# Two-layer decoder step on one core: the normalized rows kept in feature order, and the gather's weights loaded with a step of eight elements

## The chip, the cores and the metric

The kernel runs on one core of one Trainium2 chip. Its time is the device time of one execution in microseconds (us). Three executions of the kernel before took 1154.89, 1151.49 and 1144.73 us; their median, 1151.49 us, is the time before. A fourth execution was profiled. It took 1148.22 us, and its trace spans 1146.3 us from the first to the last instruction.

## The reference, cut to what matters

The model is one inference step with two layers: RWKV-7 time mixing, then differential attention, each followed by a mixture of 16 experts of which every token uses two. There are 336 tokens (272 of a prompt with its meta tokens, 64 of eight samples), a model width of 1024 and an expert width of 512, all in float32.

```python
x = _layernorm(DEEPNORM_ALPHA * x + h, post_ln[l, 0, 0], post_ln[l, 0, 1])
x = _layernorm(DEEPNORM_ALPHA * x + _moe(x, router_w, router_b, w_gate[l], w_up[l], w_down[l]), ...)

# _moe: gates are zero but for the two chosen experts of a token
for e in range(N_EXPERTS):
    h = jax.nn.silu(xt @ w_gate[e]) * (xt @ w_up[e])
    y = y + gates[:, e:e + 1] * (h @ w_down[e])
```

The change touches the way in which the normalized rows `xt` reach the experts, in both layers.

## The kernel before, in words

The program is written out engine by engine, with semaphores between them; the order on each engine is the order of its code. TensorE is PE in the profile (its weight loads are PEld), VectorE DVE, ScalarE ACT, GpSimd POOL. SP issues the weight transfers.

In each layer the 336 token rows lie in `YT`, tokens on the partitions in three tiles `t` (128, 128 and 80 rows) and 1024 features along each row. After the first layer norm (`normalize`, L2423) three things happen. PE turns the rows (L1356) for the router; ACT and DVE copy the turned rows out (`turned_copy`); and the router's small chain on DVE chooses the experts, which ends in `select`, a 0/1 matrix `SelF` that says which token goes into which of 64 places of an expert (L2460).

Beside this the rows are split into a high and a low part, `XTM[0]` and `XTM[1]`, of the type that PE multiplies in one pass (fp32r). ACT writes the high parts (`normed_copy`, L1851: tile 0 between the turned copies, tiles 1 and 2 after the router's sigmoid). The low parts, row minus high part, are written by POOL for tile 0 (`remainder`, L690) and by DVE for tiles 2 and 1 (L2515), right after `select`.

`gather` (L1212) multiplies them with `SelF`. It takes four experts at a time (a quad): for each of 8 chunks of 128 features there are 6 matmuls (two parts by three tiles), each with 128 columns of `XTM` as the stationary weights and 256 columns of `SelF` moving. A quad therefore has 48 matmuls, a layer 192, the program 384. A `gather` call takes two chunks (12 matmuls), and its result is moved out of PSUM by ACT or DVE with scale and bias (`gathered`). The four calls of a layer's first quad run before its first pair of experts; each later quad is gathered inside the loop over the eight pairs, two calls (24 matmuls) in each of the pairs 0 to 5 (`more_rows`).

A chunk's 128 features are not neighbours. The experts' weights come in with feature 8p+k on partition p, chunk k, because that makes each partition's part of a transfer contiguous. So chunk k of the gather must hold features k, k+8, k+16 and so on. Before the change the split copies do this: they write `XTM` chunk by chunk, so that consecutive features of a row land 128 elements (512 bytes) apart, and the gather's weights are 128 consecutive elements.

The weights of the experts use seven slots of 2 MB in SBUF. SP issues a half slot (1 MB) as soon as the pair that used it has finished that half (`free`, waiting for `gate_mm`, `up_mm`, `down_mm` of PE). A pair needs six slots, and PE works through a pair as gate, up, gather or scatter, turn, down.

Of the kernel before, what the change touches and what calls it, by code (L numbers as in the profile page):

```python
# [8 lines left out]
ALU = mybir.AluOpType  # L9
ACT = mybir.ActivationFunctionType  # L10
AX = mybir.AxisListType.X
F32 = mybir.dt.float32
# [4 lines left out]
P = 128  # L17
D = 1024
NC = D // P
# [20 lines left out]
QUAD = 4 * SLOTS  # L40
# [104 lines left out]
def build(nc, I, O, const, at):  # L145
    ctx = ExitStack()
    with ctx:
        sems = {}

        def S(name):  # L150
            name = SHARED.get(name, (name, 0))[0]
            if name not in sems:
                sems[name] = ctx.enter_context(nc.semaphore(name))
            return sems[name]

        A = ctx.enter_context(nc.sbuf_tensor("arena", [P, ARENA], F32))
        ps = ctx.enter_context(nc.psum_tensor("ps", [P, 8, 512], F32))
# [6 lines left out]
        def cut(n, where=None):  # L164
            if where is not None:
                return A[:, where:where + n]
            v = A[:, top[0]:top[0] + n]
            top[0] += n
            assert top[0] <= ARENA, top
            return v  # L170
# [31 lines left out]
        YT = cut(3 * D)  # L202
        xT = chan(YT[:, 0:NC * T])
        YT = YT.rearrange("p (t n) -> p t n", t=3)
# [40 lines left out]
        o = SLOT  # L245
# [3 lines left out]
        def rc(name):  # L249
# [28 lines left out]
        XTM = [[nc.alloc_sbuf_tensor_at(f"xtm_{part}{t}", [P, D], FR, offset=arena_at + 4 * (base + NC * T + D * (3 * i + t)))[:, :]  # L278
                for t in range(3)] for i, part in enumerate(("hi", "lo"))]
# [121 lines left out]
        def rx_part(i, h, c):  # L401
            return (rx_lo_[i] if h else rx_hi_)[c // 4][:, T * (c % 4):T * (c % 4) + T]

        def x_part(place, h, c):
            return PX[place][c // 4][h][:, T * (c % 4):T * (c % 4) + T]

        def bank(b, n=512):
            return ps[:, b, 0:n]

# [20 lines left out]
        def sums_bank(lv, hf):  # L430
            return (0, 2)[(lv + 1) % 2] + hf
# [197 lines left out]
        def _(pool):  # L629
# [55 lines left out]
            def remainder(l):  # L685

                pool.wait_ge(S("xtm_hi"), 3 * l + 1)
                lo, hi = [XTM[h][0].rearrange("t (k p) -> t p k", k=NC) for h in (1, 0)]
                pool.tensor_tensor(lo, YT[:, 0, :].rearrange("t (p k) -> t p k", k=NC), hi.bitcast(F32), ALU.subtract
                                   ).then_inc(S(f"first_lo{l}"), 1)  # L690

            pool.wait_ge(S("wkvp_ready"), after("wkvp_ready", 1))
# [13 lines left out]
            for hp in range(2):  # L706
                pool.memset(QZ[hp][64 * (1 - hp):64 * (1 - hp) + 64], 0.0)
                i = pool.drain()
# [56 lines left out]
        def _(pe):  # L765
            prime(pe, "pe")
            def mm(out, lhsT, rhs, start=True, stop=True):
                return pe.matmul(out, lhsT, rhs, start=start, stop=stop)  # L768

            def three(out, x, w, start, stop):  # L770

                mm(out, x[0], w[0], start, False)
                mm(out, x[1], w[0], False, False)
                return mm(out, x[0], w[1], False, stop)
# [7 lines left out]
            for t in (1, 0, 2):  # L782
                t0, n = TOK[t]
# [3 lines left out]
                for hf in range(2):  # L787
                    for c in range(4):
                        i = pe.transpose(ps[:, 1 + 2 * t + hf, n * c:n * c + n],
                                         xrow[0:n, t, P * (4 * hf + c):P * (4 * hf + c) + P], ident[0:n, 0:n])  # L790
# [63 lines left out]
            for i in range(3):  # L854
                for co in range(NC):
                    n = 8 * i + co
# [4 lines left out]
                    for k in range(NC):  # L861
                        if co == 0:
                            pe.wait_ge(S("rx_hi"), 8 * i + k + 1)
                            pe.wait_ge(S("rx_lo"), 8 * i + k + 1)
                        m = three(bank(n % 4, T), [PWR[n % 2][h][:, P * k:P * k + P] for h in range(2)],
                                  [rx_part(i, h, k) for h in range(2)], k == 0, k == NC - 1)
# [164 lines left out]
            for k in range(NCH):  # L1031
# [3 lines left out]
                for lv in range(1, LEVELS[k]):  # L1035
                    for hf in range(2):
# [3 lines left out]
                        for c in range(4 * hf, 4 * hf + 4):  # L1040
                            for hp, q in enumerate(QH):
                                m = mm(ps[QH[1 - hp], sums_bank(lv, hf), 64 * (c % 4):64 * (c % 4) + 64], LM[q, c, :], XU[k % 2][q, c, :])
                        m.then_inc(S("y_mm"), 1)
                    beside(k, lv)
                    for hf in range(2):
                        pe.wait_ge(S("y_ready"), product_at(k, lv, hf))
                        b = products_bank(lv, hf)
                        for c in range(4 * hf, 4 * hf + 4):
# [4 lines left out]
                            for hp, q in enumerate(QH):  # L1053
                                m = mm(ps[QH[1 - hp], b + 1, cols], XI[q, c, :], YI[q, c, :])
# [42 lines left out]
            for c in range(NC):  # L1097
                if c % 2 == 0:
                    pe.wait_ge(S("sq_a"), after("sq_a", c // 2 + 1))
                m = variances(c, slice(0, 256))  # L1100
# [12 lines left out]
            for c in range(NC):  # L1113
                if c % 4 == 0:
                    pe.wait_ge(S("sq_b"), after("sq_b", c // 4 + 1))
                m = variances(c, slice(256, T))
# [94 lines left out]
            def gather(q, i, order):  # L1211

                for h, t in order:
                    t0, k = TOK[t]
                    for c in (2 * i, 2 * i + 1):
                        o = QUAD * (c % 2)
                        m = mm(ps[:, i % 2, o:o + QUAD], XTM[h][t][0:k, P * c:P * c + P],
                               SelF[q % 2][0:k, t].rearrange("p e s -> p (e s)"), h == t == 0 and c == 2 * i, h == t == 1 and c == 2 * i + 1)
                if order[-1] == (1, 1):
                    m.then_inc(S("xg_mm"), 1)  # L1220

            def more_block(n0, n):
                pe.wait_ge(*over("o_sel", n, 1))
                for c in range(NC):
                    for t, (t0, k) in enumerate(TOK):
                        for h in range(2):
                            m = mm(ps[:, c // 4, P * (c % 4):P * (c % 4) + P], XTM[h][t][0:k, P * c:P * c + P],
                                   SelO[0:k, t, :], t + h == 0, t + h == 3)
                m.then_inc(S("o_pe"), 1)
                pe.wait_ge(*over("o_xg", n, 1))  # L1230
                pe.wait_ge(*over("o_weights", n, 48))
                for k in range(2):
                    w = w_in(n0 + 6 * (PAIRS - 1) + 3 + k)
                    for c in range(NC):
                        m = mm(bank(2 + k), oXg[:, c, :], w[:, c, :], c == 0, c == NC - 1)
                m.then_inc(S("o_pe"), 1)
                pe.wait_ge(*over("o_h", n, 1))
                for f in range(NF):
                    pe.transpose(ps[:, 2, P * f:P * f + P], HH[:, P * f:P * f + P], ident)
                for t, (t0, k) in enumerate(TOK):  # L1240
                    pe.transpose(ps[:, 3, t0:t0 + k], SelO[0:k, t, :].bitcast(F32), ident[0:k, 0:k])
                for t, (t0, k) in enumerate(TOK):
                    m = mm(ps[:, 3, 400:401], SelO[0:k, t, :].bitcast(F32), gtp[0:k, t:t + 1], t == 0, t == 2)
                m.then_inc(S("o_pe"), 1)
                pe.wait_ge(*over("o_ht", n, 1))
                w = w_down(n0 + 6 * (PAIRS - 1) + 5)
                for hf in range(2):
                    for f in range(NF):
                        m = mm(bank(4 + hf), oHT[:, P * f:P * f + P], w[:, f, 512 * hf:512 * hf + 512], f == 0, f == NF - 1)
                m.then_inc(S("o_pe"), 1)  # L1250
                pe.wait_ge(*over("o_y", n, 1))
                for t, (t0, k) in enumerate(TOK):
                    for hf in range(2):
                        if t:
                            pe.wait_ge(*over("o_add", n, 2 * t + hf - 1))
                        mm(ps[0:k, 6 + hf, :], oSG[:, t0:t0 + k], oYY[:, 512 * hf:512 * hf + 512]).then_inc(S("o_pe"), 1)
# [166 lines left out]
            for t, (t0, n) in enumerate(TOK):  # L1423
                pe.wait_ge(S("ln_x"), 3 + t + 1)
                for c in range(NC):
                    m = pe.transpose(ps[:, c, t0:t0 + n], YT[0:n, t, P * c:P * c + P], ident[0:n, 0:n])
# [181 lines left out]
        def _(act):  # L1608
            prime(act, "act")
            def f(out, in_, func, **k):  # L1610
                return act.activation(out, in_, func, **k)  # L1611
# [35 lines left out]
            for i, t in enumerate((1, 0, 2)):  # L1647
                t0, n = TOK[t]
# [116 lines left out]
            for n in range(24):  # L1765
                i, c = n // 8, n % 8
# [79 lines left out]
            def normed_copy(l, t):  # L1846

                n = TOK[t][1]
                if l == 0 and t == 0:
                    act.wait_ge(S("out_wkvp"), 32)  # L1850
                f(XTM[0][t][0:n, :].rearrange("t (k p) -> t p k", k=NC), YT[0:n, t, :].rearrange("t (p k) -> t p k", k=NC),  # L1851
                  ACT.Copy).then_inc(S("xtm_hi"), 1)

            def turned_copy(l, t):

# [106 lines left out]
            for i, X in enumerate((aKT, aVT, QZ)):  # L1962
                for c in range(NC):
# [8 lines left out]
                    else:  # L1972
                        if c == 0:
                            act.wait_ge(S("q_zero"), after("q_zero", 1))
                        for hp in range(2):
                            q = slice(64 * hp, 64 * hp + 64)
                            n = 32 * c + 16 * (c % 2) + SS * hp
                            copy(X[hp][q, c, :], ps[q, c % 4, 0:2 * P])
                            m = copy(Qbd[q, :, n:n + SS], ps[q, c % 4, 2 * P:T].rearrange("p (u n) -> p u n", n=SS))
# [91 lines left out]
        def _(dve):  # L2071
            prime(dve, "dve")
            tt, tsc, stt, cp = dve.tensor_tensor, dve.tensor_scalar, dve.scalar_tensor_tensor, dve.tensor_copy
# [9 lines left out]
            for i, t in enumerate((1, 0, 2)):  # L2083
                t0, n = TOK[t]
# [418 lines left out]
            def experts(l, n0):  # L2503
# [6 lines left out]
                def remainder(t):  # L2510

                    n = TOK[t][1]
                    dve.wait_ge(S("xtm_hi"), 3 * l + t + 1)
                    lo, hi = [XTM[h][t][0:n, :].rearrange("t (k p) -> t p k", k=NC) for h in (1, 0)]
                    tt(lo, YT[0:n, t, :].rearrange("t (p k) -> t p k", k=NC), hi.bitcast(F32), ALU.subtract).then_inc(S("xtm_lo"), 1)  # L2515

                def folded(t):

# [104 lines left out]
                for t in range(3):  # L2623
                    m = with_gains(t, ALPHA)
# [28 lines left out]
            for co in range(1, 24):  # L2653
# [3 lines left out]
                if 2 <= co < 5:  # L2657
                    m = with_gains(co - 2, 1.0)
# [38 lines left out]
            for u in range(NU + 2):  # L2697
                if u < NU:
                    t, h = units[u]
# [8 lines left out]
                if 1 <= u <= NU:  # L2708
                    t, h = units[u - 1]
                    nk = P * t + P  # L2710
                    st, p = st4[(u - 1) % 2], PP[(u - 1) % 3]
# [14 lines left out]
            for i in range(UNITS):  # L2726
                b = i + 2 - TAIL // SS
                n = TAIL if i < TAIL // SS else TS
# [56 lines left out]
            for t in range(3):  # L2785
                n = TOK[t][1]
                stt(centred[0:n, t, :], YT[0:n, t, :], lsum[1][0:n, t:t + 1], GB[0:n, 0, :], ALU.add, ALU.mult)
            for t in range(3):
                n = TOK[t][1]
# [32 lines left out]
```

## Time and profile before

| what | before |
|---|---|
| median of three runs | 1151.49 us |
| the profiled execution, its own time | 1148.22 us |
| its span, first to last instruction | 1146.3 us |
| PE busy | 1031.3 us, 90% |
| DVE busy | 531.3 us, 46% |
| ACT busy | 361.8 us, 32% |
| POOL busy | 72.1 us, 6% |
| expert stage of layer 0, from the first gather to the last add | about 387 to 622 us |
| expert stage of layer 1 | about 897 to 1132 us |

The busy time of an engine is the union of its instructions' durations. A matmul's duration includes the time in which the next one already runs, so the distance between two starts, and not the duration, tells how fast a row of matmuls goes. PEclk is the granted clock: 1.00 stands for 2.4 GHz and 0.50 for 1.2 GHz.

### The profile page before, as it was taken

The page shows a single profiled execution, that of the slowest core. Times are in us where ns is not written, and L with a number is a line of the kernel's source. Part 1 is how long each engine was busy: PE and PEld are TensorE (multiplying, and loading weights), DVE is VectorE, ACT ScalarE, POOL GpSimd, SP SyncE. Part 2 cuts the span into 40 slices and gives each one's busy share as a digit, 9 for nine tenths or more (in the row PEclk, how much of TensorE's full clock was granted, in tenths as well). Part 3 has the DMA queues.
Part 4 walks back from the last instruction along what each step waited for, and adds up shares of the span by engine and source line. Part 5 has one row for each costly group of instructions (what it writes and reads, how often), then busy time and mean ns, then how long its engine had stood idle before and what let it go on. Part 6 is the DMA issues. An engine that isn't in the chain of part 4 may idle for free.

```text
span 1146.3 us, 23962 instructions
## 1 busy us (share of the span) xinstructions
PE 1031.3 (90%) x10421; PEld 719.2 (63%) x10422; DVE 531.3 (46%) x1043; ACT 361.8 (32%) x734; POOL 72.1 (6%) x103
## 2 busy tenths in 40 slices
PE   5999868998998699999997899998788699999994
PEld 4888867888866444444444899876556445454532
DVE  6866546665676621212124744565445612121215
ACT  3436435443443311111113534463324211111112
POOL 3002000010000100000000011202001000000000
PEclk9999979999999899999999999999879799999998
DMA  9703020013205899999999415535745199999992
GB/s 314 263 16 74 11 59 4 4 40 114 93 2 198 362 397 423 423 423 422 421 418 387 179 37 191 186 133 192 265 177 219 53 424 423 421 423 423 423 411 91
DMA packets 58109, 273.31 MB, mean 238 GB/s; under 512 B 5185, under 2 KB 7754, under 8 KB 33938
## 3 DMA queue, kind: packets, MB, share of 16 engines
q1 hardware_dynamic: 48112, 237.45, 51.7%
q0 software_dynamic: 9264, 33.97, 9.2%
q8 instruction: 85, 1.39, 0.5%
q10 hardware_dynamic: 626, 0.32, 0.1%
q14 instruction: 22, 0.18, 0.0%
HBM read 265.29 MB, written 6.46 MB: 237 GB/s over the span
## 4 chain that ended last, share of the span: by engine, by line
PE 76%; DVE 10%; DMA 7%; issue 3%; ACT 3%; DVEq 1%; ACTq 0%; POOLq 0%; POOL 0%
PE ps L768 70%; DMA arena<-in_moe_w_up 5%; PE ps L912 1%; ACT arena L1611 1%; PE ps L1483 1%; DMA arena<-in_cache_k 1%; DVE arena L2100 1%; DMA arena<-in_const 1%; DVE arena L2408 1%; PE ps L1191 1%; PE ps L1308 1%; ACT arena L1614 1%; PE ps L1356 1%; DVE arena L2239 0%; DVE arena L2238 0%
## 5 line engine op out<-in xcount | busy, mean ns | idle before, releaser
L768 PE MATMUL ps<-arena 64*64 64x64 f32 (+11 forms) x7576 | 580.8, 317 | 44.0 <-DVE arena L2595 10.8
L768 PEld LDWEIGHTS ps<-arena 64*64 64x64 f32 (+4 forms) x7576 | 321.3, 138 | 280.3 <-issue 218.0
L1614 ACT COPY arena<-ps 128x512 f32<-128x512 f32 (+7 forms) x308 | 126.2, 430 | 305.6 <-PE ps L768 159.8
L2490 DVE TENSOR_TENSOR arena<-arena,ps 128x512 f32<-128x512 f32 x16 | 17.4, 1084 | 164.5 <-PE ps L768 164.5
L1611 ACT ACTIVATE arena<-ps,arena 128x256 f32<-128x256 f32 (+4 forms) x98 | 46.2, 504 | 125.0 <-PE ps L768 95.0
L2501 DVE SCALAR_TENSOR_TENSOR yy_lo<-ps,arena,yy_hi 128x512 fp32r<-128x512 f32 x32 | 22.7, 747 | 123.1 <-ACT yy_hi L1611 123.1
L1611 ACT ACTIVATE pw_hi<-arena 128x1024 fp32r<-128x1024 f32 x40 | 42.3, 1058 | 89.7 <-PE ps L768 89.7
L768 PE MATMUL ps<-px_hi,pw_hi 128*128 128x336 f32 x192 | 62.7, 327 | 3.5 <-DVE px_lo L2326 2.5
L768 PE MATMUL ps<-px_lo,pw_hi 128*128 128x336 f32 x192 | 60.9, 317 | 0.0
L768 PE MATMUL ps<-px_hi,pw_lo 128*128 128x336 f32 x192 | 60.7, 316 | 0.0
L1611 ACT ACTIVATE yy_hi<-ps,arena 128x512 fp32r<-128x512 f32 x32 | 20.5, 685 | 106.3 <-PE ps L768 106.3
L1611 ACT ACTIVATE arena<-arena 128x1 f32<-128x1 f32 (+7 forms) x71 | 43.1, 642 | 20.5 <-DVE arena L2397 16.3
L2315 DVE TENSOR_TENSOR pw_lo<-arena,pw_hi 128x1024 fp32r<-128x1024 f32 x24 | 29.4, 1225 | 43.1 <-ACT pw_hi L1611 43.0
L768 PE MATMUL ps<-yy_hi,sg 128*128 128x512 f32 (+1 forms) x96 | 40.4, 420 | 5.0 <-DVE arena L2477 2.7
L768 PE MATMUL ps<-pw_hi,px_hi 128*128 128x512 f32 (+1 forms) x96 | 40.7, 424 | 3.0 <-DVE px_lo L2326 3.0
L2475 DVE TENSOR_TENSOR arena<-arena,ps 128x512 f32<-128x512 f32 (+1 forms) x48 | 32.5, 684 | 23.4 <-PE ps L768 23.4
L1611 ACT ACTIVATE arena<-ps 128x512 f32<-128x512 f32 (+4 forms) x23 | 11.4, 506 | 100.3 <-PE ps L768 100.2
L2106 DVE TENSOR_TENSOR pwr_lo<-arena,pwr_hi 128x1024 fp32r<-128x1024 f32 x24 | 29.4, 1223 | 28.4 <-ACT pwr_hi L1611 28.1
L768 PE MATMUL ps<-rx_hi_hi,pwr_hi 128*128 128x336 f32 x96 | 33.4, 347 | 9.5 <-ACT rx_hi_hi L1611 4.5
L768 PEld LDWEIGHTS ps<-px_hi,pw_hi 128*128 128x128 f32 x192 | 36.2, 188 | 5.0 <-issue 2.8
L768 PE MATMUL ps<-pw_hi,px_lo 128*128 128x512 f32 (+1 forms) x96 | 39.2, 408 | 0.0
L768 PE MATMUL ps<-pw_lo,px_hi 128*128 128x512 f32 (+1 forms) x96 | 39.0, 406 | 0.0
(230 smaller groups left out, 1378.3 us busy)
## 6 DMA issues: line engine op xcount, KB each, us to landing
arena<-in_moe_w_gate SPq DMA_DIRECT2D x64, 1024.0 KB, 15.3
arena<-in_moe_w_up SPq DMA_DIRECT2D x64, 1024.0 KB, 18.2
arena<-in_moe_w_down SPq DMA_DIRECT2D x64, 1024.0 KB, 17.4
arena<-in_rwkv_w_rkv SPq DMA_DIRECT2D x5, 2048.0 KB, 20.8
arena<-in_w_kv_shared SPq DMA_DIRECT2D x4, 2048.0 KB, 20.2
arena<-in_cache_k POOLq DMA_DIRECT2D x16, 512.0 KB, 4.5
arena<-in_cache_v POOLq DMA_DIRECT2D x16, 512.0 KB, 6.6
arena<-in_rwkv_w_out SPq DMA_DIRECT2D x2, 2048.0 KB, 10.7
```

Source lines behind the costliest of these rows:

```text
L768: return pe.matmul(out, lhsT, rhs, start=start, stop=stop)
L912: m = pe.transpose(ps[:, b + hf, P * c:P * c + P], src[:, 4 * hf + c, o0:o0 + P], ident)
L1191: m = pe.transpose(ps[0:n, 4 + g % 4, P * c:P * c + P], X[:, 4 * hf + c, t0:t0 + n], ident)
L1308: m = pe.transpose(ps[:, 2, P * f:P * f + P], HH[:, P * f:P * f + P], ident)
L1356: m = pe.transpose(ps[:, 2 * t + hf, n * c:n * c + n], YT[0:n, t, P * (4 * hf + c):P * (4 * hf + c) + P], ident[0:n, 0:n])
L1611: return act.activation(out, in_, func, **k)
L1614: return act.copy(out, in_)
L2106: tt(lo, w_in(L_RKV + n // 4)[:, :, P * (n % 4):P * (n % 4) + P], hi.bitcast(F32), ALU.subtract).then_inc(S("rw_lo"), 1)
L2315: tt(lo, w_in(L_KV + co // 4)[:, :, P * (co % 4):P * (co % 4) + P], hi.bitcast(F32), ALU.subtract).then_inc(S("pw_lo"), 1)
L2475: tt(YT[0:n, t, h], YT[0:n, t, h], ps[0:n, 6 + i % 2, :], ALU.add).then_inc(S("add_done"), 1)
L2490: tt(HH.rearrange("p (k q) -> p q k", k=NF), HS.rearrange("p (q k) -> p q k", k=NF), bank(3).rearrange("p (q k) -> p q k", k=NF), ALU.mult ...
L2501: stt(YY[ROWS[j]][1][:, h], bank(4 + hf), gsl, YY[ROWS[j]][0][:, h].bitcast(F32), ALU.mult, ALU.subtract).then_inc(S("yl_ready"), 1)
```

## The change

The split copies now write `XTM` in the order of `YT`, so all three engines read and write contiguous rows. The gather, and the overflow block that handles an expert with more than 64 tokens, read their 128 weight columns from the same rows with a step of eight elements (32 bytes). Every engine has the same instructions in the same order as before, with the same waits; on PE, 384 weight loads have another access pattern, and on ACT, DVE and POOL six, four and two copies.

```diff
@@ helpers
+        def spread(x, c):
+
+            return x.rearrange("t (p k) -> t k p", k=NC)[:, c, :]
@@ POOL, remainder(l)
-                lo, hi = [XTM[h][0].rearrange("t (k p) -> t p k", k=NC) for h in (1, 0)]
-                pool.tensor_tensor(lo, YT[:, 0, :].rearrange("t (p k) -> t p k", k=NC), hi.bitcast(F32), ALU.subtract
+                pool.tensor_tensor(XTM[1][0], YT[:, 0, :], XTM[0][0].bitcast(F32), ALU.subtract
                                    ).then_inc(S(f"first_lo{l}"), 1)
@@ PE, gather(q, i, order)
-                        m = mm(ps[:, i % 2, o:o + QUAD], XTM[h][t][0:k, P * c:P * c + P],
+                        m = mm(ps[:, i % 2, o:o + QUAD], spread(XTM[h][t][0:k, :], c),
                                SelF[q % 2][0:k, t].rearrange("p e s -> p (e s)"), h == t == 0 and c == 2 * i, h == t == 1 and c == 2 * i + 1)
@@ PE, more_block(n0, n)
-                            m = mm(ps[:, c // 4, P * (c % 4):P * (c % 4) + P], XTM[h][t][0:k, P * c:P * c + P],
+                            m = mm(ps[:, c // 4, P * (c % 4):P * (c % 4) + P], spread(XTM[h][t][0:k, :], c),
                                    SelO[0:k, t, :], t + h == 0, t + h == 3)
@@ ACT, normed_copy(l, t)
-                f(XTM[0][t][0:n, :].rearrange("t (k p) -> t p k", k=NC), YT[0:n, t, :].rearrange("t (p k) -> t p k", k=NC),
-                  ACT.Copy).then_inc(S("xtm_hi"), 1)
+                f(XTM[0][t][0:n, :], YT[0:n, t, :], ACT.Copy).then_inc(S("xtm_hi"), 1)
@@ DVE, remainder(t)
-                    lo, hi = [XTM[h][t][0:n, :].rearrange("t (k p) -> t p k", k=NC) for h in (1, 0)]
-                    tt(lo, YT[0:n, t, :].rearrange("t (p k) -> t p k", k=NC), hi.bitcast(F32), ALU.subtract).then_inc(S("xtm_lo"), 1)
+                    tt(XTM[1][t][0:n, :], YT[0:n, t, :], XTM[0][t][0:n, :].bitcast(F32), ALU.subtract).then_inc(S("xtm_lo"), 1)
```

## Rows read from the trace of the kernel before

**Rows 1.** The page: span, and PE and DMA in 40 slices.

```profile
span 1146.3 us, 23962 instructions
PE   5999868998998699999997899998788699999994
DMA  9703020013205899999999415535745199999992
```

**Rows 2.** Windows in layer 0's expert stage: busy per engine (instructions), clock, DMA, GB/s.

```profile
420.00:440.00 20.00, 20.00 (x119) 10.36 (x117) 3.50 (x5) 3.47 (x6) 0.00 (x0) 1.00 1.01 422
...
580.00:600.00 20.00, 18.45 (x87) 7.68 (x88) 3.38 (x6) 2.71 (x6) 0.18 (x1) 1.00 1.01 418
```

**Rows 3.** Waits of PE for weights, 569 to 626 us: total us, times, longest.

```profile
PE ps L768 <- DMA arena<-in_moe_w_up: 0.9, 1, 0.9
...
PE ps L768 <- DMA arena<-in_moe_w_gate: 0.3, 1, 0.3
```

**Rows 4.** The same view, 1050 to 1131 us.

```profile
PE ps L768 <- DMA arena<-in_moe_w_up: 0.6, 1, 0.6
```

**Rows 5.** Timeline, pair 0 of layer 0: start us, us; the gather's 24 matmuls between.

```profile
410.57 0.98 PE L768 MATMUL ps<-sel,xtm_hi 128*128 128x256 f32 x6
...
413.54 0.60 PE L1308 MATMUL ps<-arena 128*128 128x128 f32 x4
```

**Rows 6.** Matmuls that read `XTM`: ns min/median/max, first and last start.

```profile
L768 PE MATMUL ps<-sel,xtm_hi x192: 278/283/553, 387.0 to 1060.9; 128*128 128x256 f32 x128, 80*128 80x256 f32 x64
L768 PE MATMUL ps<-sel,xtm_lo x192: 279/283/415, 388.5 to 1061.7; 128*128 128x256 f32 x128, 80*128 80x256 f32 x64
```

**Rows 7.** Timeline, first 24 gather matmuls: first and last group of layer 0.

```profile
387.05 1.62 PE L768 MATMUL ps<-sel,xtm_hi 128*128 128x256 f32 x6 [1.49 <-DVE sel L2460]
...
390.17 1.36 PE L768 MATMUL ps<-sel,xtm_lo 128*128 128x256 f32 x10
```

**Rows 8.** Windows: layer 0's first gather, up to its last ten matmuls.

```profile
387.00:390.20 3.20, 3.15 (x15) 3.18 (x16) 3.20 (x2) 0.00 (x0) 0.00 (x0) 0.51 1.01 420
```

**Rows 9.** Timeline, last group of layer 1's first 24 gather matmuls.

```profile
900.09 2.28 PE L768 MATMUL ps<-sel,xtm_lo 128*128 128x256 f32 x10
```

**Rows 10.** Timeline of PEld at 392.4 us: two weight loads in a row.

```profile
392.40 0.30 PEld L768 LDWEIGHTS ps<-sel,xtm_hi 128*128 128x128 f32 x2 [1.08 <-ACT arena L1611]
```

**Rows 11.** Weight loads by form: busy us, mean ns | idle before.

```profile
L768 PEld LDWEIGHTS ps<-arena 64*64 64x64 f32 x3776 | 88.4, 136 | 26.6 <-issue 13.2 <-DVE arena L2239 8.0 <-ACT arena L1614 2.4
...
L768 PEld LDWEIGHTS ps<-yy_hi,sg 128*128 128x128 f32 x64 | 12.0, 187 | 17.9 <-issue 16.5
```

**Rows 12.** Split copies of 128x1024, by form: written 512 bytes apart, and contiguously.

```profile
L1611 ACT ACTIVATE xtm_hi<-arena 128x1024 fp32r<-128x1024 f32 x4 | 7.9, 1979 | 0.4 <-DMA out_new_wkv_prompt<-arena 0.4
...
L1611 ACT ACTIVATE pw_hi<-arena 128x1024 fp32r<-128x1024 f32 x40 | 42.3, 1058 | 89.7 <-PE ps L768 89.7
...
L2515 DVE TENSOR_TENSOR xtm_lo<-arena,xtm_hi 128x1024 fp32r<-128x1024 f32 x2 | 3.9, 1974 | 0.0
...
L2106 DVE TENSOR_TENSOR pwr_lo<-arena,pwr_hi 128x1024 fp32r<-128x1024 f32 x24 | 29.4, 1223 | 28.4 <-ACT pwr_hi L1611 28.1 <-DVEq L2296 0.2
```

**Rows 13.** DVE sums over 128 elements: read 64 bytes apart (L2533), and contiguously.

```profile
L2533 DVE TENSOR_REDUCE arena<-arena 128x16 f32<-128x128 f32 x2 | 0.7, 372 | 0.1
...
L2668 DVE TENSOR_REDUCE arena<-arena 128x2 f32<-128x128 f32 x1 | 0.3, 286 | 0.1
```

**Rows 14.** Timeline, layer 0 before routing: high copy, turn of tile 2, logits of tile 1.

```profile
373.07 2.05 ACT L1611 ACTIVATE xtm_hi<-arena 128x1024 fp32r<-128x1024 f32 x1 [0.35 <-DMA out_new_wkv_prompt<-arena]
...
374.26 0.77 PE L1356 MATMUL ps<-arena 80*128 80x80 f32 x8 [0.20 <-DVE arena L2423]
...
375.60 0.64 PE L768 MATMUL ps<-arena 128*32 128x128 f32 x16 [0.56 <-DVE arena L2508]
```

**Rows 15.** Weight loads of transposes, by form: mean ns by 128 and 16 columns.

```profile
L1191 PEld LDWEIGHTS ps<-arena 128*128 128x128 f32 x32 | 4.0, 141 | 0.1
...
L1191 PEld LDWEIGHTS ps<-arena 128*16 128x16 f32 x16 | 1.4, 89 | 0.4
```

## The prediction, as it stood before the changed kernel was run

> **What bounds the kernel now.** I read the page first: PE is busy in nearly every slice, and in the two expert stages (slices 15 to 21 and 32 to 40) the DMA engines are full as well [rows 1]. Which of the two sets the pace there is read from windows of the stage: PE 20.00 of 20.00 us busy and 422 GB/s at the same time [rows 2]. The waits decide. In the whole of layer 0's stage PE waited for weights only at its end, 0.9 and 0.3 us [rows 3]; in layer 1 it waited 0.6 us [rows 4]. Seven full slots give PE a lead at the start, PE uses it up, and both arrive at the last pair together. So in these stages a matmul made faster is worth almost nothing, because the weights would then be late; one made slower counts in full, but for 1.2 and 0.6 us.
>
> The gather is part of PE's work there. Its 24 matmuls of pair 0 start at 410.57, and the next matmul starts at 413.54 [rows 5]: 2.97/24 = 0.124 us each. There are 384 such matmuls [rows 6].
>
> **What the change takes away.** All six ACT copies, four DVE and two POOL subtractions become contiguous. ACT's took 1979 ns, and a contiguous one of the same size takes 1058; DVE's 1974 against 1223 [rows 12]. Most of this gives nothing, since the work is covered:
> - ACT's copies of tiles 1 and 2 run beside the router chain, which ends later on DVE. POOL's subtraction is long done when `select` ends.
> - DVE's two subtractions run beside the first 14 gather matmuls. The matmuls that read their result stand in the last ten, which in layer 0 start at 390.17 and follow each other without a gap [rows 7]. Without that cover a shorter subtraction would be worth 2 x 0.75 = 1.5 us a layer.
> - ACT's copy of tile 0 is on the path in layer 0. It stands ahead of the turned copy that the logits of tile 1 wait for: PE ended the turn of tile 2 at 374.26 + 0.77 = 375.03 and began the logits at 375.60 [rows 14]. The copy ends 0.9 us earlier, so PE and the chain behind it gain 0.57 us. In layer 1 PE comes to that place later and nothing is gained. Together **-0.6 us**.
>
> **What it adds.** No instruction is added or moved and no wait changes; the only price is in 384 weight loads that read elements 32 bytes apart. No load of the kernel before does that, so its price must be bounded.
>
> A contiguous load first. When both weight buffers are free, two loads of 128 columns take 0.30 us [rows 10]; less one load's own 0.19 [rows 11] they start 0.11 us apart. The columns say the same: (187 - 136) ns for 64 more columns [rows 11] is 0.80 ns each, 102 ns for 128. A load of 0.11 us beside a pace of 0.124 is only just hidden. Any real lengthening shows.
>
> Now the step. An element written 512 bytes from the last one cost ACT (1979 - 1058)/1024 = 0.90 ns more, and DVE (1974 - 1223)/1024 = 0.73 ns [rows 12]. Reading alone does it too: a DVE sum over 128 elements that lie 64 bytes apart took 372 ns, a contiguous one 286 [rows 13], 0.67 ns more each. So a strided element costs 0.67 to 0.90 ns on two engines, in reads and writes. For 128 columns that is 86 to 115 ns. Below it lies nothing, if PE's load path does not mind the step; above it, twice as much, if a column is read twice; both are rivals. I take 0.82 ns, the middle of ACT's and DVE's large copies, since they are averages over 1024 elements: **105 ns** a load. The load then takes 0.215 us and is longer than the matmul beside it, so the pace becomes 0.124 + 0.105 = 0.229 us.
>
> What the rows show stops at steps of 64 bytes. The Trainium skill, "Advanced Engine Details and Errata", section SBUF Cachelines, says that SBUF has 16-byte lines and that an access which goes to a new line each time pays a penalty; it names no engine. By it a step of 32 bytes pays like the longer ones and the term stands; by a step that is still short enough to be free, it would be zero. No row here shows 32 bytes.
>
> Where the matmuls run at the half clock they are slow already. Layer 0's first gather has a granted clock of 0.51 until 390.2 [rows 8], and its first 14 matmuls take 390.17 - 387.05 = 3.12 us [rows 7], 0.223 each, about the strided load. I count those at nothing, and at 105 ns for the upper end. In layer 1 all of the first 24 are of that kind: the last ten take 2.28 us [rows 9].
>
> **The sum.** Layer 0: the last 10 of the first 24, the other 24 of the first quad, and 24 in each of six pairs (144): 178 x 0.105 = 18.7 us. Layer 1: 24 + 144 = 168, 17.6 us. Less the waits for weights that PE no longer has, 1.2 + 0.6, and less 0.6 for ACT's copy: 18.7 + 17.6 - 1.8 - 0.6 = **+33.9 us**. Nothing else hides it. In the stretch of [rows 5] the turn that follows starts at once, so the gather already lasts longer than the ACT and DVE work it covers. The first quad's gather also holds back the first freed slot, and with it the whole stream of weights, by some 3 us; PE is later by six times that at the end, so it does not wait.
>
> Against the profiled execution's own 1148.22 us this gives 1182.1. That execution is 3.3 us under the median of the three runs, so the forecast for a median is 1151.5 + 33.9 = **1185 us**, 2.9% slower.
>
> Its own range: 86 ns give 346 x 0.086 - 2.4 = +27.4, 115 ns with the 38 slow-clock matmuls give 346 x 0.115 + 38 x 0.105 - 2.4 = +41.4; with the spread of the runs (-6.8, +3.4) 1172 to 1196.
>
> **The rivals.**
> *The load does not mind the step (chance 0.20).* A load spends 0.80 ns on a column, while a transpose's spends (141 - 89)/112 = 0.46 [rows 15]. So an ordinary fp32r load leaves its read path idle nearly half the time, and that slack may take up the step. Against it: ACT and DVE, with different contiguous times, end near the same strided one, 1.93 and 1.93 ns per element (1979/1024 and 1974/1024 [rows 12]), which looks like the memory and not the engine. It decides at a load of about 0.12 us: up to there the matmul hides it. Then only ACT's 0.6 us is left: 1151 us, 1145 to 1155 with the spread. The Trainium skill, "TensorE: Matmul & The Clock Gate", section LDWEIGHTS, makes the time of a load depend on its number of columns alone; by that rule this rival holds, and the change is not slower.
>
> *Each column is read twice (0.11).* The two steps per column of the rows just named may be two reads, each with its own 105 ns: 346 x 0.210 + 38 x 0.105 - 2.4 = +74 us, 1226 us. For it: the factor 0.80/0.46. Against it: nothing says that the second step goes to memory again.
>
> *The clock falls (0.05).* During the longer gathers the array multiplies less than half the time. If the granted clock fell in each of the twelve bursts of 24 and the matmuls behind ran at half pace for as long as a burst takes now, 12 x 2.97/2 to 12 x 2.97 = 18 to 36 us come on top: about 1212 us. Against it: nothing but the pace of one kind of matmul changes.
>
> **How the numbers follow.** The forecast has 0.64. Its own range holds 0.9 of that, 0.58. To hold 8 in 10 the range reaches down over the first rival (1145) and up to the lower part of the clock rival (1206): 0.60 + 0.19 + 0.02. The double read is left out. About 1% (11.5 us) is what a measurement here can tell from no change. Slower by more than that: 0.64 + 0.11 + 0.05, less a little for a load only slightly longer, 0.79. Within it: the first rival, 0.19. Faster: 0.02, as no row offers more than the 1.5 us a layer above.
>
> **What would show it.** In the profile after: the weight loads of `XTM` near 0.30 us (0.19 now), their matmuls 0.23 us apart in pairs 0 to 5, the copies of ACT near 1.06 and of DVE near 1.23 us, no waits for `in_moe_w_up` at the end of either stage, and GB/s in the stage below 422. The forecast is wrong if the loads keep 0.19 us, or if the pace grows and PE's end does not move, which would mean that the weights and not PE set the stage.

## The result and the profile after

The changed kernel took 1193.81 us (median of 4 runs, 1190.32 to 1203.71), the kernel before 1148.11 us (4 runs, 1141.87 to 1154.89). The ratio on record is 1.0441 with a 95% interval of [1.0403, 1.0479]: **4.4% slower**. Divided as they stand, the two medians give 1.040, 45.7 us; the record does not say where the difference comes from, and both say slower. The time lies inside the range and on the forecast side, 9 us over the forecast of 1185. The profiled execution took 1193.12 us; its span grew from 1146.3 to 1191.2 us, by 44.9, where the forecast had 33.9.

The page, span, PE, granted clock and DMA in 40 slices (slices 14 to 22 and 32 to 40 hold the two expert stages):

```profile
span 1191.2 us, 23962 instructions
...
PE   5998787998996999999998999898796999999994
...
PEclk8999979999998789998999899999888899998998
DMA  9703200131109699998999215526815499999981
```

The number of instructions is that of [rows 1]. In the stages the DMA row, all nines from slice 15 to 22 and from 33 to 39 before, now has an 8 in slices 19 and 39; the clock row has an 8 in slices 15, 19 and 37, nines before.

Pair 0 of layer 0 on PE, which answers to [rows 5] (start, duration; the 24 gather matmuls lie between):

```profile
417.15 1.72 PE L771 MATMUL ps<-sel,xtm_hi 128*128 128x256 f32 x6
...
423.14 1.05 PE L1311 MATMUL ps<-arena 128*128 128x128 f32 x4
```

(423.14 - 417.15)/24 = 0.250 us a matmul, 0.124 before. The twelve such bursts inside the loop took 5.89 to 6.08 us, 2.97 to 3.07 before. The weight loads of the high parts, before and after, and the copies, which answer to [rows 12] (ns min/median/max, first and last start):

```profile
L768 PEld LDWEIGHTS ps<-sel,xtm_hi x192: 186/192/333, 387.0 to 1060.8; 128*128 128x128 f32 x128, 80*128 80x128 f32 x64
...
L771 PEld LDWEIGHTS ps<-sel,xtm_hi x192: 312/338/344, 387.5 to 1107.9; 128*128 128x128 f32 x128, 80*128 80x128 f32 x64
...
L1614 ACT ACTIVATE xtm_hi<-arena x6: 1050/1052/1063, 373.1 to 912.8; 128x1024 fp32r<-128x1024 f32 x4, 80x1024 fp32r<-80x1024 f32 x2
...
L2516 DVE TENSOR_TENSOR xtm_lo<-arena,xtm_hi x4: 1212/1215/1216, 387.3 to 921.1; 80x1024 fp32r<-80x1024 f32 x2, 128x1024 fp32r<-128x1024 f32 x2
```

The copies became as short as announced. The loads went from 192 ns (median) to 338.

All waits of PE in 380 to 650 us, layer 0's stage (total us, times, longest), against [rows 3]:

```profile
PE ps L771 <- DVE arena L2596: 5.6, 1, 5.6
PE ps L771 <- DVE sel L2462: 1.5, 1, 1.5
PE ps L771 <- DVE arena L2479: 1.4, 2, 1.1
PE ps L771 <- DVE arena L2477: 1.1, 2, 0.7
PE ps L771 <- issue: 1.1, 1, 1.1
PE ps L771 <- ACT arena L1614: 0.6, 1, 0.6
```

No row names a weight any more: PE alone sets the stage now. Windows of that stage, beside [rows 2] (busy and count per engine, clock, DMA share, GB/s):

```profile
440.00:460.00 20.00, 20.00 (x105) 13.54 (x103) 2.07 (x3) 2.71 (x6) 0.00 (x0) 1.00 1.01 426
...
423.20:429.50 6.30, 6.30 (x30) 4.24 (x30) 1.00 (x2) 1.09 (x3) 0.00 (x0) 0.50 0.98 412
...
551.90:555.80 3.90, 3.90 (x11) 1.18 (x12) 0.99 (x2) 0.00 (x0) 0.00 (x0) 0.50 0.92 389
556.00:560.00 4.00, 4.00 (x22) 1.39 (x20) 0.00 (x0) 0.00 (x0) 0.00 (x0) 1.00 0.43 111
```

In the last row the DMA engines move 111 GB/s; the profile's waits put SP's pauses in issuing expert weights down to PE, 40 of them in 380 to 660 us, so DMA now waits for PE to free a slot. Over 400 to 580 us the rate is 374 GB/s, 416 before, though single windows still show 426. The 423.20 and 551.90 rows show what the forecast had at zero: directly behind a burst, or in its last part, the granted clock is 0.50, the lower of the two levels, 1.2 GHz, and PE starts 11 matmuls in 3.9 us, where it starts 22 in the 4.0 us that follow. Such stretches lie behind three of the twelve loop bursts; in the trace of before behind none.

**Where the 44.9 us lie.** All starts of PE in the two stages were sorted by kind and by the granted clock, and the distances to the next start were added up (before, after):

| | layer 0 | layer 1 |
|---|---|---|
| stage, first gather matmul to last scatter | 235.7, 261.4 | 236.2, 257.9 |
| the 192 gather matmuls | 27.7, 49.9: +22.2 | 28.5, 49.7: +21.2 |
| 512-column matmuls at half clock | 0, 28: +5.4 | 0, 18: +3.2 |
| small matmuls at half clock | +1.1 | 0 |
| 512-column matmuls at full clock | 0.2211, 0.2171 each: -3.0 | -2.7 |
| sum | +25.7 | +21.7 |

The rest of the program was 2.5 us shorter; the part between the stages lies between 269.0 and 274.2 us in the traces of this case, so this is its spread. Together 25.7 + 21.7 - 2.5 = +44.9.

### The profile page after: what moved, and what is told of

Same layout as the page of the kernel before. It is cut to its first block, busy times and chain, and to the rows that moved or that the text cites. A ratio compares the mean times of both kernels' runs of the same rounds, so it can differ in the third digit from the quotient of the medians.

```text
span 1191.2 us, 23962 instructions
## 1 busy us (share of the span) xinstructions
PE 1079.3 (91%) x10421; PEld 766.3 (64%) x10422; DVE 527.9 (44%) x1043; ACT 357.0 (30%) x734; POOL 72.1 (6%) x103
## 4 chain that ended last, share of the span: by engine, by line
PE 81%; DVE 9%; issue 3%; ACT 3%; DMA 2%; DVEq 1%; ACTq 0%; POOLq 0%; POOL 0%
PE ps L771 76%; PE ps L915 1%; ACT arena L1614 1%; DMA arena<-in_cache_k 1%; PE ps L1486 1%; DVE arena L2102 1%; PE ps L1311 1%; DVE arena L2410 1%; DMA arena<-in_const 1%; PE ps L1194 1%; PE ps L1359 1%; ACT arena L1617 0%; DVE arena L2210 0%; DVE arena L2241 0%; DVE arena L2240 0%
## 5 line engine op out<-in xcount | busy, mean ns | idle before, releaser
L771 PE MATMUL ps<-sel,xtm_hi 128*128 128x256 f32 (+1 forms) x192 | 53.9, 426 | 4.6 <-DVE sel L2462 3.3
L771 PEld LDWEIGHTS ps<-sel,xtm_hi 128*128 128x128 f32 (+1 forms) x192 | 49.2, 337 | 11.8 <-issue 10.0
L2468 DVE TENSOR_SCALAR arena<-ps,arena 128x256 f32<-128x256 f32 x32 | 15.9, 540 | 84.5 <-PE ps L771 84.5
L771 PE MATMUL ps<-sel,xtm_lo 128*128 128x256 f32 (+1 forms) x192 | 52.1, 414 | 0.0
L771 PEld LDWEIGHTS ps<-sel,xtm_lo 128*128 128x128 f32 (+1 forms) x192 | 49.6, 339 | 0.0
```

What stands on the lines that cost most here:

```text
L2468: m = tsc(Xg[q % 2][:, c, :], ps[:, i % 2, QUAD * (c % 2):QUAD * (c % 2) + QUAD], turn_gb[q // 4][0][:, c:c + 1], turn_gb[q // 4][1][:, c: ...
```

## The experiments

All ratios are those on record, against the kernel before on the same chip, with the 95% interval; the quotients of the medians differ from them by up to 0.4 points.

**Steps of two and four elements.** Both keep everything of the change but the place of a feature in the row. Groups of `STEP` features stay together, and the load's step is `STEP` elements.

```diff
+STEP = 2
 def spread(x, c):
-    return x.rearrange("t (p k) -> t k p", k=NC)[:, c, :]
+    return x.rearrange("t (j p i) -> t j i p", j=NC // STEP, i=STEP)[:, c // STEP, c % STEP, :]
@@ the copies of ACT, DVE, POOL: written "t (j p i) -> t p j i", read "t (p j i) -> t p j i"
```

> The split copies write pairs of elements, and the gather's weights are read with a step of two elements (8 bytes). Theory (a load pays when each element stands in a 16-byte stretch of its own): two elements share one, so the load stays near 0.19 us, the gather's pace at 0.124 us, the copies near ACT 1.06 and DVE 1.22 us, and the time within 1% of before. Rival (any step but one costs): pace 0.24 us as in the changed kernel, and 35 to 50 us more than before.

> As the run with a step of two, but with runs of four elements and a step of four (16 bytes). Theory: every element is in a stretch of its own, so the price is that of eight: pace 0.24 to 0.25 us, ratio to before 1.035 to 1.048. Rival (the price grows with the distance): half of it, pace near 0.18 us, 15 to 25 us more than before.

Step 2 (8 bytes): 1145.09 us, ratio 1.0004 [0.9978, 1.0030]. Step 4 (16 bytes): 1182.61 us, ratio 1.0321 [1.0274, 1.0369], a little under what was expected (1.035 to 1.048). Loads and copies at step 2, and its burst of pair 0:

```profile
L780 PEld LDWEIGHTS ps<-sel,xtm_hi x192: 193/196/332, 391.4 to 1065.0; 128*128 128x128 f32 x128, 80*128 80x128 f32 x64
...
L1623 ACT ACTIVATE xtm_hi<-arena x6: 1079/1096/1124, 372.8 to 893.6; 128x1024 fp32r<-128x1024 f32 x4, 80x1024 fp32r<-80x1024 f32 x2
```
```profile
417.27 0.99 PE L780 MATMUL ps<-sel,xtm_hi 128*128 128x256 f32 x6
...
420.26 0.60 PE L1320 MATMUL ps<-arena 128*128 128x128 f32 x4
```

The same at step 4:

```profile
L780 PEld LDWEIGHTS ps<-sel,xtm_hi x192: 307/329/338, 388.5 to 1101.2; 128*128 128x128 f32 x128, 80*128 80x128 f32 x64
```
```profile
417.64 1.68 PE L780 MATMUL ps<-sel,xtm_hi 128*128 128x256 f32 x6
...
423.36 0.60 PE L1320 MATMUL ps<-arena 128*128 128x128 f32 x4
```

2.99/24 = 0.125 at 8 bytes, 5.72/24 = 0.238 at 16, 0.246 at 32. A step as such costs nothing here, and 32 bytes cost hardly more than 16: the jump lies between 8 and 16 bytes. Step 2 keeps ACT's gain (1096 ns) at no cost on PE and still is no faster, since the time that ACT and DVE save is covered.

**Only the high parts with the step.** The low parts are written chunk by chunk as before, from the feature-ordered high parts, and loaded contiguously. So half of the loads go back to 128 neighbours.

```diff
@@ gather and the overflow block
-  spread(XTM[h][t][0:k, :], c)
+  (spread(XTM[0][t][0:k, :], c) if h == 0 else XTM[1][t][0:k, P * c:P * c + P])
@@ the two subtractions: all three operands as "t (k p) -> t p k" (low) and "t (p k) -> t p k" (row, high)
```

> Only the high parts are in feature order and read with a step of eight; the low parts are written and read as before. Theory (each strided load costs about 0.12 us more, and PE's pace is the stage's): half of the gather's growth, 22 us, and fewer drops of the granted clock, so 1.5 to 2.5% more than before. Rival (the time is lost to the granted clock, which falls once a gather is slow at all): nearly all of the loss remains, over 3%.

1163.59 us, ratio 1.0154 [1.0098, 1.0210]. Both kinds of load in one trace, and a burst of pair 1:

```profile
L772 PEld LDWEIGHTS ps<-sel,xtm_hi x192: 312/338/348, 386.0 to 1078.5; 128*128 128x128 f32 x128, 80*128 80x128 f32 x64
...
L772 PEld LDWEIGHTS ps<-sel,xtm_lo x192: 187/192/336, 387.4 to 1079.3; 128*128 128x128 f32 x128, 80*128 80x128 f32 x64
```
```profile
439.14 1.72 PE L772 MATMUL ps<-sel,xtm_hi 128*128 128x256 f32 x6
...
443.57 0.60 PE L1312 MATMUL ps<-arena 128*128 128x128 f32 x4
```

4.43/24 = 0.185: twelve matmuls at 0.246 and twelve at 0.124 give 4.44. The price hangs on the load itself, not on its neighbours. The clock fell behind none of these twelve bursts, and the kernel lost 18 us against before, under half of the 45; the interval is clear of no change, though not of 2%.

**The kernel before with fewer matmuls.** The low parts are left out of the gather in the quads 1 to 3 of both layers (so the gathered rows there carry the high parts alone): 144 matmuls fewer, or 17.9 us of PE.

```diff
@@ gather of the kernel before
+  last = (0, 2) if q % 4 else (1, 1)
   for h, t in order:
+      if q % 4 and h:
+          continue
...                      # the last matmul is (h, t) == last
```

> The kernel before, without the low parts in the gathers inside the loop (the last three quads of each layer): 72 matmuls a layer fewer, 72 x 0.124 = 8.9 us of PE. Theory (PE and the stream of weights arrive together): PE then waits for weights and the time falls by at most 3 us a layer, within 0.6% of before. Rival (PE alone sets the stage): 18 us less, 1.5% faster.

1144.90 us, ratio 1.0003 [0.9982, 1.0023]. Waits of PE for weights in layer 0's stage (400 to 625 us):

```profile
PE ps L768 <- DMA arena<-in_moe_w_up: 4.1, 3, 1.7
...
PE ps L768 <- DMA arena<-in_moe_w_gate: 1.9, 1, 1.9
```

In layer 1 they are 4.4 and 2.0 us. PE's saving turned into waits for weights, which the profile counts from a matmul's modelled end and so too short, and behind two of these waits the clock fell as well (557.9 to 561.3 and 1073.3 to 1076.7 us). The stages stayed at 236.0 and 235.8 us (235.7 and 236.2 before). So the weights set a floor at the very place where the kernel before stands: slack in one direction only, as the prediction had it.

**The changed kernel once more**, with no edit.

> The changed kernel once more, for its granted clock. Theory (the strided load reads at the pace of the memory and not of TensorE): the gather's pace is 0.246 us in every burst of the loop and 0.25 us in the first gather at the half clock too; the drops of the granted clock behind the bursts lie elsewhere than in the first profile and cost 5 to 12 us in sum, and the ratio to before is 1.040 to 1.048. Rival (the drops belong to the kernel's fixed order): the same drops at the same pairs.

1189.02 us (1182.77 to 1196.90), ratio 1.0413 [1.0342, 1.0483]. The stages are 256.8 and 257.9 us, all paces the same (0.246 to 0.249), and the low clock lies at other pairs: behind pairs 2 and 3 of layer 0 and pair 2 of layer 1, here one of them (columns as above). By the sorting above it cost some 6 us:

```profile
479.90:483.30 3.40, 3.40 (x14) 2.93 (x15) 0.43 (x1) 1.00 (x2) 0.00 (x0) 0.50 1.01 422
```

The load's price repeats to the nanosecond (312/338/344 again); which pairs the clock falls behind does not. Behind the first quad it fell in both layers of both traces, and the sixteen 512-column matmuls there took 5.15 us instead of 3.45. The clock may be a good part of why this kernel's runs spread over 14 us and those of before beside it over 8 (1140.04 to 1147.60).

**Steps of three, six and one, in one kernel.** Layer 1's quads 1, 2 and 3 load columns with these steps, and so other features than the reference's.

```diff
+def weights_of(x, q, c):
+    step = {5: 3, 6: 6, 7: 1}.get(q, 8)
+    first = P * c if step == 1 else c
+    return x[:, first:first + 127 * step + 1:step]
...                      # used in gather in place of spread(x, c)
```

> The changed kernel; in layer 1 the gather's weights are read with another step in three quads: 3 elements (quad 1), 6 (quad 2), 1 (quad 3), so these quads take other features than the reference and the last layer's output is not the reference's. Theory (a load pays for each 16-byte stretch that it touches): 0.246 us for 6, 0.124 for 1, and for 3, which touches 96 stretches with 128 elements, 96/128 of the strided load, a pace near 0.18 us. Rival (a load pays for its distance in bytes): 6 dearer than 4 and cheaper than 8 by steps, 3 between 2 and 4 in a straight line, 0.18 as well, but 6 clearly under 0.246.

The bursts with step 3 and step 6 (one execution, 1174.74 us):

```profile
969.23 1.33 PE L777 MATMUL ps<-sel,xtm_hi 128*128 128x256 f32 x6
...
973.59 0.60 PE L1317 MATMUL ps<-arena 128*128 128x128 f32 x4
...
1029.62 1.64 PE L777 MATMUL ps<-sel,xtm_hi 128*128 128x256 f32 x6
...
1035.21 0.60 PE L1317 MATMUL ps<-arena 128*128 128x128 f32 x4
```

4.36/24 = 0.182 and 5.59/24 = 0.233 us; step 1 gave 0.124. Count the 16-byte stretches that 128 columns touch: 96 at step 3, 128 at steps 4, 6 and 8. The paces are 1.89, 1.86, 1.82 and 1.92 ns for each stretch. At step 2 there are 64, 0.12 us by this price, just under the 0.124 of the matmul beside it. So a load that is not hidden pays for stretches, not for distance: 96 of them cost three quarters of 128, and six is not dearer than four. That steps 4, 6 and 8 differ by 5% among themselves stays open.

**Can the load be hidden? First try: single gather matmuls between the down matmuls.** The second gather call of each pair is dealt out, one or two matmuls behind every four half-array matmuls (64 columns of weights, 512 moving) of the down projection.

```diff
@@ more_rows: only the first of the two gather calls
@@ down projection
+  between = rest_of_rows()      # yields the 12 matmuls of the second call
   for hf in range(2):
       m = down(f, hf)
+      for _ in range(2 if hf == 0 else 1):
+          next(between, None)
```

> The changed kernel, with every second gather call of the loop (12 of its 24 matmuls a pair, 72 a layer) placed one or two at a time between the 512-column matmuls of the pair's down projection. Theory (the strided load is seen only where it outlasts the matmul beside it): these matmuls cost PE about 0.12 to 0.15 us each instead of 0.246, 7 to 9 us a layer less than the changed kernel, so 1.026 to 1.034 of before. Rival (a strided load holds PE up wherever it stands): no gain, 1.040 to 1.048.

It came out the other way: 1233.33 us, ratio 1.0790 [1.0746, 1.0834], slower than the change itself. To tell the placing from the step, the kernel before got the same placing with its contiguous loads:

> The kernel before (contiguous weights) with the same placing of every second gather call between the matmuls of the down projection that made the changed kernel slower, where one such matmul cost about 0.58 us instead of 0.246. Theory (the price is that of changing between half-array and full-array matmuls, and the strided load is hidden there): the same 0.55 to 0.6 us for a single one with contiguous weights, and the two kernels differ by the bursts that were left alone, 72 x 0.121 = 8.7 us a layer, and the first quad's 4 us. Rival (a strided load is not hidden there either): 0.12 us less for each of the 72, so 0.46 us, and the two kernels differ by over 35 us.

1183.56 us, ratio 1.0351 [1.0314, 1.0388]. PE in both, the strided loads first (start, duration):

```profile
421.97 1.08 PE L771 MATMUL ps<-arena 128*64 128x512 f32 x4
422.98 0.51 PE L771 MATMUL ps<-sel,xtm_hi 128*128 128x256 f32 x1
423.42 1.08 PE L771 MATMUL ps<-arena 128*64 128x512 f32 x4
```
```profile
415.31 1.08 PE L768 MATMUL ps<-arena 128*64 128x512 f32 x4
416.32 0.39 PE L768 MATMUL ps<-sel,xtm_hi 128*128 128x256 f32 x1
416.63 1.08 PE L768 MATMUL ps<-arena 128*64 128x512 f32 x4
```

From one group of four to the next: 1.45 us strided, 1.32 contiguous. The four take 4 x 0.217 = 0.87 us, so even the contiguous single matmul costs 0.45 us there, against 0.124 in a burst; the placing was the mistake. Where two stand together (1.69 and 1.44 us from group to group) the second costs 0.24 and 0.12 us, as in a burst, so the placing is paid once for each change from half-array to full-array matmuls and back. And the single strided one costs 0.13 us more than the contiguous one, as much as in a burst: its load hides behind nothing there. That is the rival of the second run, 0.46 us and over 35 us between the kernels: their medians lie 49.8 us apart, on two chips. Why the load does not hide stays open.

**Second try: longer matmuls.** In layer 1 the gather of quad 1 (strided) and of quad 2 (contiguous) moves 512 columns instead of 256, the same ones twice, so that a matmul should last about as long as a strided load (the results of these two quads are meaningless).

```diff
+chosen = chosen.unsqueeze(1).to_broadcast([k, 2, QUAD])      # q in (5, 6)
-m = mm(ps[:, i % 2, o:o + QUAD], spread(XTM[h][t][0:k, :], c),
+m = mm(ps[:, i % 2, :], XTM[h][t][0:k, P * c:P * c + P] if q == 6 else spread(XTM[h][t][0:k, :], c), chosen,
...                      # quad 3 as in the changed kernel
```

> The changed kernel; in layer 1 the gather's matmuls have 512 moving columns (the 256 of SelF twice) in quads 1 and 2, with the weights at a step of eight in quad 1 and contiguous in quad 2; quad 3 is as in the changed kernel. The copies of the result are meaningless, so the last layer's output is not the reference's. Theory (the load runs beside the matmul and is seen only where it is longer): both quads have a pace near 0.23 to 0.25 us, at most 0.015 apart, though their loads differ by 0.12, and quad 3 keeps 0.246. Rival (the strided load and the matmul do not run side by side): quad 1 near 0.35 us, quad 2 near 0.23.

```profile
975.37 1.85 PE L771 MATMUL ps<-sel,xtm_hi 128*128 128x512 f32 x6
...
981.48 0.60 PE L1315 MATMUL ps<-arena 128*128 128x128 f32 x4
...
1037.46 1.66 PE L771 MATMUL ps<-sel,xtm_hi 128*128 128x512 f32 x6
...
1043.14 0.60 PE L1315 MATMUL ps<-arena 128*128 128x128 f32 x4
```

6.11/24 = 0.255 strided, 5.68/24 = 0.237 contiguous (one execution, 1190.58 us): 0.018 apart, where 256 columns leave 0.122. That is slightly more than expected, but nearly all of the price is gone. Loads that start 0.24 us apart when they follow each other hide behind full-array matmuls of that length; at 256 columns the matmul is too short for that.

**The clock, over all traces.** The granted clock fell in or directly behind 15 of the 52 loop bursts whose matmuls of 256 columns stood 0.233 to 0.255 us apart (the change 3 of 12 and 3 of 12, step 4 1 of 12, step 6 1 of 2, the step-8 bursts of the two kernels with mixed quads 3 of 6 and 4 of 8). It fell behind none of the 44 others (before 12, step 2 12, high parts alone 12, steps 3 and 1 4, 512 columns 4). The 512-column bursts among these are as long as the strided ones, 5.68 and 6.11 us, with the array multiplying nearly throughout (0.217 us of each matmul). Nor did it fall behind the twelve bursts of only 12 strided matmuls, 3.0 us each, in the first try above. Its one fall in that kernel's stages came behind a pause of PE of 1.14 us, the two falls in the kernel with fewer matmuls behind waits for weights. So the fall goes with long bursts in which PE is shown busy but mostly waits for its weights. The two were seen together; that one causes the other is not shown, since no kernel kept the strided loads and held the clock up in another way.

No version beat the kernel before; step 2 equals it within 0.3%.

## Why the prediction was right, and where its size was off

- **The number** was right with some luck. The profiled span grew by 44.9 us, above the +27.4 to +41.4 that the prediction worked out; the median came to lie inside 1172 to 1196 by the allowance for the spread of the runs. The gather and the clock came out higher than forecast, the waits and the rest of the program lower, and the errors partly cancel.
- **The bound** held. PE slower counts in full, PE faster gives waits: +45 us on one side, 1.0003 on the other.
- **The load term** was the right step and too small: 0.105 us was taken, and the loop bursts grew by 2.96 us, 0.123 a matmul. By the forecast's own counts 178 + 168 = 346 this is 42.7 us instead of 36.3. The step that failed is the price per column: 0.82 ns, the middle of ACT's and DVE's extras, with 115 ns a load as the upper bound. Loads that follow each other freely start 0.24 us apart, before 0.11, so the extra is 0.13/128 = 1.0 ns a column, more than either engine's. Of its sources, [rows 13] compares sums with 16 and with 2 results, so its 0.67 ns is not the step's alone. A second slip went the other way and hid a part of the first: the extra was added to the pace (0.229), although a load longer than the matmul is the pace itself. With the prediction's own load of 0.215 us the term would have been 346 x 0.091 = 31.5 us, so its 36.3 was nearer by luck. Had ACT's full time been used and not its extra, 1979/1024 = 1.93 ns an element [rows 12], 128 columns would have given 0.247 us; the pace measured is 0.246. That is said afterwards, and steps 4 and 6 gave 0.238 and 0.233.
- **The matmuls at the half clock**, counted at nothing: the first 14 of layer 0 take 391.09 - 387.51 = 3.58 us, before 3.12 [rows 7]:

```profile
387.51 1.81 PE L771 MATMUL ps<-sel,xtm_hi 128*128 128x256 f32 x6 [1.49 <-DVE sel L2462]
...
391.09 2.67 PE L771 MATMUL ps<-sel,xtm_lo 128*128 128x256 f32 x10
394.38 1.81 PE L771 MATMUL ps<-sel,xtm_hi 128*128 128x256 f32 x6 [0.62 <-ACT arena L1614]
```

  That is 0.256 us each at the half clock, near the 0.246 at the full: the load's time hardly changed with the granted clock. The table's gather rows hold 43.4 us, 42.7 of them in the term above, so this was worth 0.7 us in all.
- **The waits for weights** gave back 3.0 + 2.7 us, not 1.8. Taken in order and at the full clock, sixteen 512-column matmuls need the same time in both kernels to within 0.1 us, but for the last pairs before the change (from 587 us on in layer 0, 1080 us in layer 1): there PE waited. [rows 3, 4] show less because a wait is counted from the modelled end of a matmul: the matmul ahead of the 0.9 us of [rows 3] starts 1.46 us before the next one, where the pace is 0.217, and another wait of that kind in layer 1 has no row at all.
- **ACT's 0.6 us** did not show. The turned tile came late, because the clock had fallen already (371.5 to 374.9 us, before and after, columns as in the windows above; then the timeline after):

```profile
371.50:374.90 3.40, 3.20 (x40) 2.64 (x40) 3.07 (x6) 2.96 (x5) 0.00 (x0) 1.00 1.02 423
371.50:374.90 3.40, 3.40 (x20) 3.07 (x22) 2.34 (x5) 2.52 (x6) 0.61 (x1) 0.50 1.02 425
...
373.15 1.06 ACT L1614 ACTIVATE xtm_hi<-arena 128x1024 fp32r<-128x1024 f32 x1 [0.30 <-DMA out_new_wkv_prompt<-arena]
...
375.37 0.78 PE L1359 MATMUL ps<-arena 80*128 80x80 f32 x8
...
376.07 0.64 PE L771 MATMUL ps<-arena 128*32 128x128 f32 x16
```

  Against [rows 14] the copy is 1 us shorter, but PE's own turn ends at 375.37 + 0.78 = 376.15, so the logits now follow PE's own turn without a gap. Whether the gain would show at the full clock stays open. The first gather starts at 387.51 instead of 387.05; in the other traces of this study it starts between 383.5 and 391.4, far more spread than the term.
- **The clock**, a rival with 0.05, came true in part: 5.4 + 1.1 + 3.2 = 9.7 us, with stretches behind 3 of 12 loop bursts and the first quads, where the rival had all twelve and 18 to 36 us. Its argument "nothing but the pace of one kind of matmul changes" was no argument against it. Forecast and measured sum: 36.3 - 1.8 - 0.6 = 33.9; 43.4 - 5.7 + 9.7 - 2.5 = 44.9.
- **The rivals.** That the load does not mind the step is refuted by 338 against 192 ns. The Trainium skill's rule in "TensorE: Matmul & The Clock Gate", section LDWEIGHTS, that the number of columns alone counts, does not hold here: all of these loads have 128. That a column is read twice is refuted by a pace of 0.246 where it needed 0.33. The Trainium skill's "Advanced Engine Details and Errata", section SBUF Cachelines, adds that at least two hits on a 16-byte line are needed to absorb the latency; the traces agree for PE's loads, free beside this matmul at 8 bytes (0.125) and not at 16 (0.238).

## What to carry to other kernels

Moving a stride from a copy that nobody waits for onto the weight loads of the engine that sets the end is a bad trade, however much the copy gains; ask of both sides who waits. Price a load by its own full time against the matmul beside it, not by an extra on top of the pace, since only what exceeds the matmul counts. If a strided load must be, keep pairs of fp32 elements together, and look at the granted clock of the work behind it.

## What was not expected of the hardware

- Where elements lie 12 bytes or more apart, a weight load's pace follows the 16-byte stretches that it touches, 1.82 to 1.92 ns each, at the full clock, and hardly changes at the half clock (0.246 and about 0.25 us for 128 columns at a step of eight).
- A trace in which PE is busy for 100% of a window can hold matmuls that mostly wait for their weights; the granted clock fell in or behind 15 of 52 such bursts of 24, and its low stretches, those behind the first quads included, cost up to 6.5 us a layer.
- One full-array matmul set between half-array ones cost 0.45 us, 0.124 in a row of its own kind; a second one beside it cost 0.12.
